# Attention lanes in fewer steps, another order of column groups, and VectorE's chunks of w_ada moved towards w_o

## The chip, the cores and the metric

The kernel runs on 1 core of one Trainium2 chip. The metric is the device time of one execution in microseconds (us); lower is better. The five engines of the core are TensorE (PE; its weight loads are listed apart as PEld), VectorE (DVE), ScalarE (ACT), GpSimd (POOL) and SyncE (SP, which only issues the DMA transfers here).

## The reference

Two transformer blocks run one after the other on x of 256 tokens by 2048 features, all in float32. The change lies in the first block alone:

```
mod = silu(c) @ w_ada + b_ada            # w_ada 2048 x 12288, six chunks of 2048: shift, scale, gate (twice)
h = rms_norm(x) * (1 + scale_a) + shift_a
proj = h @ w_in                          # 2048 x 5456: d_q, d_k, d_v, s_q, s_k, s_v, i_q, i_k, i_w
q, k, i_q, i_k = partial_rope(...)       # rotates the first quarter of each head
diff_out = rms_norm((softmax(q1 k1') - lam * softmax(q2 k2')) v)      # 8 heads, causal
dsa_out  = softmax over the top 64 keys of each query, by the indexer's scores   # 8 heads
x = x + gate_a * rms_norm([diff_out, dsa_out] @ w_o)
x = x + gate_f * rms_norm((silu(h w_gate) * (h w_up)) w_down)
```

The second block (w_in_2, MLA attention, a gated convolution, w_o_mla_2, w_o_conv_2, w_out_2) is not touched.

## The kernel before

**Chunks.** Every weight matrix is streamed from HBM in chunks of 512 rows by 512 columns (1 MB, four row blocks of 128). `chunk_plan` (from L52) writes the order of all chunks by hand. SP loads chunk c into slot c mod 5 of `raw` as soon as the slot's last chunk has been consumed (L2460 and what stands around it). A chunk of kind "lin" is used in two units (halves). For each unit ACT writes `whi`, the weights rounded to fp32r (L1039), DVE writes `wlo`, the remainder (L1648), and PE makes 12 matmuls from the pair (L566, L567, L568: hi by hi, lo by hi, hi by lo). ACT and DVE work two units ahead of PE (`AHEAD`), and there are three buffers for the pair (`NHL`), so that whi of unit i waits until PE has done unit i-3.

**w_ada.** The product with `silu(c)` is a vector times a matrix. The chunks of the column groups in `ADA_ON_PE` are multiplied on PE. Those of groups 8 to 19 ("ada" chunks here), four for each group, are multiplied and added up by DVE in `ada_step`: four instructions of 128x512 for each chunk (L1628, L1631) and one sum for each group (L1640). They are laid between the lin chunks: `BETWEEN` and `BETWEEN_LAST` say how many follow each of the first column groups of w_in, and `more` in `chunk_plan` spreads the others by `W_IN_SHARE` (over the 24 chunks of `W_IN_ORDER`) and `W_O_SHARE` (over w_o). When a group has been summed, `take` hands it to PE (L501, L502 or L506) and DVE (`mod`: L1610, L1612).

**First block.** w_in's column groups 10, 8, 9, 0, 2 are run first, a quarter of the rows at a time (`WIN_ITEMS`; DVE adds each quarter up in L1786). Then follow six column groups with all rows (`W_IN_ORDER`), then w_o. What follows the projection is done in lanes, generators that each engine's program advances by one step after each unit (`Walk.tick`). Lane 0 holds the indexer and the sparse attention of head pairs (0, 1), then (2, 3), lane 1 the differential attention of heads 0 to 3, then 4 to 7. `lane_jobs` says which column groups each needs before it is started. All engines walk through the same steps, each with its own work in them. The steps for one item of `attention` are: scores (PE L650, L653), maxima and exponentials (DVE L1874, L1876; ACT L1168), combine (DVE L2042 to L2048) with the turn of the next item, the transposes of the exponentials (PE L663 to L665, copied by ACT L1061 and DVE L1918), weigh (PE L673 to L676). Then comes finish (DVE L2057 copies a differential head out of PSUM to P1, after which ACT squares it in L1263; DVE L2021 for a sparse pair). Ahead of an attention stand the rotations (`rope`, DVE L1862 to L1865), two multiplications by the cosines and two by the sines, a difference and a sum, done for each token half (tb) by itself, a step for each.

w_o needs the lanes' results. Where they are not there, `Walk.until` runs steps with no unit beside them ("empty steps" here). The code of it in the tensor program:

```
need.wait_ge(m.s_dnorm, k.until(("d", 0)))
mix_operand(0, k.spare())
...
linear("w_o", 512, 512, ..., ks=(0,), s=sets[1], end=False)
linear("w_o", 0, 512, ..., ks=(8,), s=sets[0], begin=False, end=False)
need.wait_ge(m.s_dnorm, k.until(("d", 4)))
linear("w_o", 512, 512, ..., ks=(8,), s=sets[1], begin=False, end=False)
```

`mix_operand` turns a quarter of the attention's result (PE L582) and splits it (ACT L1084/L1086, DVE L1684/L1686). After each group of w_o's columns `post_group` squares it (ACT L1300) and multiplies it by the gate (DVE L2095).

## Time and profile before

| | |
|---|---|
| median of 3 runs | 2469.38 us (2468.66 to 2470.6) |
| the profiled execution, its time | 2470.69 us |
| its span | 2469.3 us |
| granted TensorE clock, mean | 0.969 |
| PE busy | 2314.2 us (94%) |
| DVE busy | 1408.0 us (57%) |
| ACT busy | 1059.2 us (43%) |
| DMA | 505.68 MB, mean 205 GB/s |

"Span" is the time from the first to the last instruction. "Busy" is the time in which an engine executes. The profile's waits name the instruction that waited, the one that released it, and the sum, count and longest of the waits. The clock of a stretch is the share of 2.4 GHz that was granted: 1.00 is 2.4 GHz throughout, 0.50 is 1.2 GHz, what lies between is a mixture of the two.

### The profile page before, as it was taken

The page shows a single profiled execution, that of the slowest core. Times are in us where ns is not written, and L with a number is a line of the kernel's source. Part 1 is how long each engine was busy: PE and PEld are TensorE (multiplying, and loading weights), DVE is VectorE, ACT ScalarE, POOL GpSimd, SP SyncE. Part 2 cuts the span into 40 slices and gives each one's busy share as a digit, 9 for nine tenths or more (in the row PEclk, how much of TensorE's full clock was granted, in tenths as well). Part 3 has the DMA queues.
Part 4 walks back from the last instruction along what each step waited for, and adds up shares of the span by engine and source line. Part 5 has one row for each costly group of instructions (what it writes and reads, how often), then busy time and mean ns, then how long its engine had stood idle before and what let it go on. Part 6 is the DMA issues. An engine that isn't in the chain of part 4 may idle for free.

```text
span 2469.3 us, 26356 instructions
## 1 busy us (share of the span) xinstructions
PE 2314.2 (94%) x10768; PEld 1875.1 (76%) x10768; DVE 1408.0 (57%) x1963; ACT 1059.2 (43%) x1461; POOL 0.7 (0%) x5
## 2 busy tenths in 40 slices
PE   5888968888999999999999899999999999999998
PEld 2665657666878888888888787888888888888886
DVE  1459888666667455455445554545554554554554
ACT  2422434434443444443444555555434444444443
POOL 0000000000000000000000000000000000000000
PEclk8998989888999999999999999999999999999999
DMA  8888757645577566555555464544565556556553
GB/s 300 336 318 301 247 197 265 219 156 185 184 275 264 198 233 213 187 193 195 188 188 191 142 195 145 162 145 154 174 200 189 188 183 197 187 187 200 188 187 138
DMA packets 255454, 505.68 MB, mean 205 GB/s; under 512 B 9077, under 2 KB 19662, under 8 KB 254182
## 3 DMA queue, kind: packets, MB, share of 16 engines
q1 hardware_dynamic: 255334, 504.00, 60.8%
q8 instruction: 85, 1.39, 0.2%
q14 instruction: 35, 0.29, 0.0%
HBM read 499.77 MB, written 4.19 MB: 204 GB/s over the span
## 4 chain that ended last, share of the span: by engine, by line
PE 82%; DVE 10%; ACT 3%; DMA 3%; issue 2%; SPq 0%; DVEq 0%; ACTq 0%
PE bank L566 25%; PE bank L568 25%; PE bank L567 25%; DVE wlo L1648 3%; DVE acc L1631 3%; PE bank L582 2%; PE bank L650 1%; DMA raw<-in_w_in_dram 1%; DMA raw<-in_w_ada_dram 1%; ACT whi L1039 1%; PE bank L520 1%; PE bank L590 1%; DVE x L1700 0%; DVE isc L1970 0%; ACT Ex_b L1168 0%
## 5 line engine op out<-in xcount | busy, mean ns | idle before, releaser
L1648 DVE TENSOR_TENSOR wlo<-raw,whi 128x1024 fp32r<-128x1024 f32 (+2 forms) x760 | 911.7, 1205 | 906.0 <-ACT whi L1039 905.4
L1039 ACT ACTIVATE whi<-raw 128x1024 fp32r<-128x1024 f32 (+2 forms) x760 | 790.2, 1044 | 1055.8 <-PE bank L568 954.0
L566 PE MATMUL bank<-whi,Ahi 128*128 128x512 f32 (+2 forms) x2304 | 916.0, 398 | 37.0 <-DVE wlo L1648 21.5
L567 PE MATMUL bank<-wlo,Ahi 128*128 128x512 f32 (+2 forms) x2304 | 900.8, 391 | 0.0
L568 PE MATMUL bank<-whi,Alo 128*128 128x512 f32 (+2 forms) x2304 | 900.2, 391 | 0.0
L566 PEld LDWEIGHTS bank<-whi,Ahi 128*128 128x128 f32 x2304 | 440.5, 191 | 142.1 <-DVE wlo L1648 30.4
L568 PEld LDWEIGHTS bank<-whi,Alo 128*128 128x128 f32 x2304 | 439.6, 191 | 91.1
L567 PEld LDWEIGHTS bank<-wlo,Ahi 128*128 128x128 f32 x2304 | 440.9, 191 | 84.5
L1631 DVE SCALAR_TENSOR_TENSOR acc<-raw,cs,acc 128x512 f32<-128x512 f32 x224 | 153.1, 746 | 0.0
L566 PE MATMUL bank<-whi,Fhi 128*128 128x512 f32 x352 | 137.7, 391 | 0.0
L568 PE MATMUL bank<-whi,Flo 128*128 128x512 f32 x352 | 137.0, 389 | 0.0
L567 PE MATMUL bank<-wlo,Fhi 128*128 128x512 f32 x352 | 137.0, 389 | 0.0
L566 PE MATMUL bank<-whi,Bhi 128*128 128x512 f32 x256 | 101.1, 395 | 0.0
L568 PE MATMUL bank<-whi,Blo 128*128 128x512 f32 x256 | 99.8, 390 | 0.0
L567 PE MATMUL bank<-wlo,Bhi 128*128 128x512 f32 x256 | 99.7, 390 | 0.0
L566 PEld LDWEIGHTS bank<-whi,Fhi 128*128 128x128 f32 x352 | 66.1, 188 | 14.1 <-issue 0.8
L568 PEld LDWEIGHTS bank<-whi,Flo 128*128 128x128 f32 x352 | 66.1, 188 | 14.0
L567 PEld LDWEIGHTS bank<-wlo,Fhi 128*128 128x128 f32 x352 | 66.1, 188 | 13.6
L568 PEld LDWEIGHTS bank<-whi,Blo 128*128 128x128 f32 x256 | 48.1, 188 | 10.3
L520 PE MATMUL bank<-raw,cs 128*32 128x512 f32 x256 | 37.6, 707 | 19.4 <-DMA raw<-in_w_ada_dram 19.4
L566 PEld LDWEIGHTS bank<-whi,Bhi 128*128 128x128 f32 x256 | 48.1, 188 | 10.0 <-issue 0.3
L567 PEld LDWEIGHTS bank<-wlo,Bhi 128*128 128x128 f32 x256 | 48.1, 188 | 9.6
(291 smaller groups left out, 1372.8 us busy)
## 6 DMA issues: line engine op xcount, KB each, us to landing
raw<-in_w_in_dram SPq DMA_DIRECT2D x156, 1024.0 KB, 5.0
raw<-in_w_ada_dram SPq DMA_DIRECT2D x96, 1024.0 KB, 5.1
raw<-in_w_gate_dram SPq DMA_DIRECT2D x44, 1024.0 KB, 5.1
raw<-in_w_up_dram SPq DMA_DIRECT2D x44, 1024.0 KB, 5.1
raw<-in_w_down_dram SPq DMA_DIRECT2D x44, 1024.0 KB, 5.0
raw<-in_w_o_dram SPq DMA_DIRECT2D x16, 1024.0 KB, 5.4
raw<-in_w_o_mla_dram SPq DMA_DIRECT2D x16, 1024.0 KB, 4.9
raw<-in_w_o_conv_dram SPq DMA_DIRECT2D x16, 1024.0 KB, 4.9
```

Source lines behind the costliest of these rows:

```text
L520: ins = pe.matmul(m.bank[b][32 * jj:32 * jj + 32, :], m.cs32[:, 4 * j + jj, :], m.raw[:, c % NRAW, jj, :], start=(j == 0), stop=(j == 3))
L566: pe.matmul(o, a_hi, w_hi, start=beg, stop=False)
L567: pe.matmul(o, a_hi, w_lo, start=False, stop=False)
L568: ins = pe.matmul(o, a_lo, w_hi, start=False, stop=fin)
L582: ins = pe.matmul(o, i, m.diag[:, tb, :], start=True, stop=True) if scaled else pe.transpose(o, i, m.ident)
L590: ins = pe.transpose(m.bank[b][:, tb * P:tb * P + P], src(tb), m.ident)
L650: pe.matmul(m.bank[ln.bank[mm]][:, PART[tb]], l, r, start=(i == 0), stop=False, skip_group_check=True)
L1039: act.activation(m.whi[:, i % NHL, :, 0:n], m.raw[:, c % NRAW, 2 * h:2 * h + 2, 0:n], ACT.Copy).then_inc(m.s_hi, 1)
L1631: ins = dve.scalar_tensor_tensor(out=o, in0=w, scalar=col, in1=o, op0=ALU.mult, op1=ALU.add)
L1648: dve.tensor_tensor(m.wlo[:, i % NHL, :, 0:n], m.raw[:, c % NRAW, 2 * h:2 * h + 2, 0:n], m.whi[:, i % NHL, :, 0:n].bitcast(F32), ALU.subtr ...
```

## The change

1. `rope` rotates both token halves in one instruction instead of one each; it takes one step where there were two, and the scratch tile `rt` grows from 256 to 272 columns for it. The two small copies of the indexer (w32, ik2) are merged in the same way.
2. The lanes have fewer steps ahead of the attention: the indexer 2 instead of 5, sparse 1 instead of 3, differential 2 instead of 5.
3. A differential head is copied out of PSUM by ACT (in `finish`, ahead of its squares) and no longer by DVE.
4. `W_IN_ORDER` becomes 4, 6, 1, 3, 5, 7.
5. `BETWEEN_LAST` goes from (2, 2, 2, 2, 2) to (1, 1, 1, 1, 2), `W_IN_SHARE` from 28 to 26, `W_O_SHARE` from 10 to 15. Of the 48 ada chunks of groups 8 to 19, 10 were in the last quarter of the first column groups, 28 in `W_IN_ORDER` and 10 in w_o. Now it is 6, 26 and 16.
6. `post_group` waits for the gate columns of its own group alone.

The diff, with what the steps above name:

```
@@ -35,11 +35,11 @@
 ROW = 2048
 
 W_IN_FIRST = (10, 8, 9, 0, 2)
-W_IN_ORDER = (4, 1, 6, 3, 5, 7)
-
-BETWEEN, BETWEEN_LAST = (3, 3, 2, 0, 0), (2, 2, 2, 2, 2)
-W_IN_SHARE = 28
-W_O_SHARE = 10
+W_IN_ORDER = (4, 6, 1, 3, 5, 7)
+
+BETWEEN, BETWEEN_LAST = (3, 3, 2, 0, 0), (1, 1, 1, 1, 2)
+W_IN_SHARE = 26
+W_O_SHARE = 15
 THIRDS = ((0, 4), (4, 8), (8, 11))
 
 
@@ -415,7 +415,7 @@
         self.skT = sb("skT", [P, S])
         self.rl = sb("rl", [P, 768])
         self.sqj = sb("sqj", [P, P])
-        rt = sb("rt", [P, 4, 256])
+        rt = sb("rt", [P, 4, 272])
         self.lane = [Lane(sb, "a", rt, (4, 5), sem), Lane(sb, "b", rt, (6, 7), sem)]
         self.ik2 = self.isc[:, 0, :].rearrange("p (t a d) -> p t a d", t=2, a=2)
         self.iwk = self.rl[:, 0:S]
@@ -711,11 +711,8 @@
         b0, b1 = ln.bank
         yield
         yield
-        yield
-        yield
-        yield
-        need.wait_ge(ln.s_rope, 4)
-        for _ in range(4):
+        need.wait_ge(ln.s_rope, 2)
+        for _ in range(2):
             k.up(ln.s_rope)
         turn_pair(b0, lambda tb: m.P1[:, tb, C_SK:C_SK + 128])
         need.wait_ge(m.s_ik, 1)
@@ -749,9 +746,7 @@
 
     def sparse(i, pairs):
         ln = m.lane[i]
-        for _ in range(2):
-            rope = k.up(ln.s_rope)
-            yield
+        rope = k.up(ln.s_rope)
         yield
         while "bias" not in k.mixed:
             yield
@@ -774,10 +769,9 @@
     def differential(i, heads):
         ln = m.lane[i]
         lo = heads[0]
-        for _ in range(4):
+        for _ in range(2):
             rope = k.up(ln.s_rope)
             yield
-        yield
 
         def turn(h):
             need.wait_ge(ln.s_rope, rope)
@@ -1216,7 +1210,7 @@
     def indexer(i):
         ln = m.lane[i]
         b0, b1 = ln.bank
-        for _ in range(5):
+        for _ in range(2):
             yield
         sk, ik = k.use(b0), k.use(b1)
         yield
@@ -1240,11 +1234,10 @@
         k.mixed["bias"] = True
 
     def sparse(i, pairs):
+        yield
+        while "bias" not in k.mixed:
+            yield
         ln = m.lane[i]
-        for _ in range(3):
-            yield
-        while "bias" not in k.mixed:
-            yield
         yield from attention(ln, pairs, 128 ** -0.5, 2, lambda hp: 8, lambda hp, pv: None)
         for hp in pairs:
             k.mixed["s", hp] = ln.bank[1], k.uses[ln.bank[1]]
@@ -1252,12 +1245,14 @@
     def differential(i, heads):
         ln = m.lane[i]
         lo, hi = heads[0], heads[-1] + 1
-        for _ in range(5):
+        for _ in range(2):
             yield
 
         def finish(h, pv):
-            need.wait_ge(m.freed[ln.bank[1]], pv)
+            b = ln.bank[1]
             c0 = C_DQ + 128 * h
+            copy_out(m.P1[:, :, c0:c0 + 128], b, pv, m.bank[b][:, 0:256].rearrange("p (t d) -> p t d", t=2))
+            need.wait_ge(m.freed[b], pv)
             for tb in range(2):
                 need.wait_ge(m.s_a, a.n)
                 a.up(act.activation(m.sqj[:, :], m.P1[:, tb, c0:c0 + 128], ACT.Square, accum_out=m.ss16[:, tb, h, 0:1]))
@@ -1848,15 +1843,14 @@
     need.wait_ge(m.s_shlo, 8)
     rt_at = [(m.s_lam, 1)]
 
-    def rope(tb, c0, h, d, half_d, tcol, ln, *cgs):
+    def rope(c0, h, d, half_d, tcol, ln, *cgs):
 
         for cg in cgs:
             released(*k.P_at[cg])
-        x = m.P1[:, tb, c0:c0 + h * d].rearrange("p (h d) -> p h d", d=d)
-        x1, x2 = x[:, :, 0:half_d], x[:, :, half_d:2 * half_d]
-        c = m.cos[:, tb, tcol:tcol + half_d].unsqueeze(1).broadcast_to([P, h, half_d])
-        sn = m.sin[:, tb, tcol:tcol + half_d].unsqueeze(1).broadcast_to([P, h, half_d])
-        r = [ln.rt[:, i, 0:h * half_d].rearrange("p (h d) -> p h d", d=half_d) for i in range(4)]
+        x = m.P1[:, :, c0:c0 + h * d].rearrange("p t (h d) -> p t h d", d=d)
+        x1, x2 = x[:, :, :, 0:half_d], x[:, :, :, half_d:2 * half_d]
+        c, sn = (t[:, :, tcol:tcol + half_d].unsqueeze(2).broadcast_to([P, 2, h, half_d]) for t in (m.cos, m.sin))
+        r = [ln.rt[:, i, 0:2 * h * half_d].rearrange("p (t h d) -> p t h d", t=2, d=half_d) for i in range(4)]
         need.wait_ge(*rt_at[0])
         for o, p1, p2 in ((r[0], x1, c), (r[1], x2, sn), (r[2], x2, c), (r[3], x1, sn)):
             v.up(dve.tensor_tensor(o, p1, p2, ALU.mult))
@@ -1900,7 +1894,7 @@
         for n, h in enumerate(items):
             if taken:
                 mod(*taken)
-            if n:
+            if n and finish:
                 finish(items[n - 1], (n - 1) % 2, sc, pv)
             sc = k.use(b0), k.use(b1)
             yield
@@ -1925,28 +1919,20 @@
             yield
         if taken:
             mod(*taken)
-        finish(items[-1], (len(items) - 1) % 2, sc, pv)
+        if finish:
+            finish(items[-1], (len(items) - 1) % 2, sc, pv)
 
     def indexer(i):
         ln = m.lane[i]
         b0, b1 = ln.bank
-        for tb in range(2):
-            rope(tb, C_IQ, 17, 64, 8, 0, ln, 8, 9, 10)
-            yield
-        for tb in range(2):
-            rope(tb, C_SK, 1, 128, 16, 8, ln, 8)
-        yield
-        for tb in range(2):
-            v.up(dve.tensor_scalar(m.w32[:, tb, :], m.P1[:, tb, C_IW:C_IW + 16], 1.0 / 32.0, None, ALU.mult))
-        need.wait_ge(ln.s_rope, 4)
-        for tb in range(2):
-            for j in range(2):
-                ins = dve.tensor_copy(m.ik2[:, tb, j, :], m.P1[:, tb, C_IK:C_IK + 64])
-                if tb + j < 2:
-                    v.up(ins)
-        ins.then_inc(m.s_ik, 1)
+        rope(C_IQ, 17, 64, 8, 0, ln, 8, 9, 10)
+        yield
+        rope(C_SK, 1, 128, 16, 8, ln, 8)
+        v.up(dve.tensor_scalar(m.w32[:, :, :], m.P1[:, :, C_IW:C_IW + 16], 1.0 / 32.0, None, ALU.mult))
+        need.wait_ge(ln.s_rope, 2)
+        dve.tensor_copy(m.ik2[:, :, :, :], m.P1[:, :, C_IK:C_IK + 64].unsqueeze(2).broadcast_to([P, 2, 2, 64])).then_inc(
+            m.s_ik, 1)
         settle()
-        yield
         yield
         k.use(b0), k.use(b1)
         yield
@@ -2005,9 +1991,7 @@
 
     def sparse(i, pairs):
         ln = m.lane[i]
-        for tb in range(2):
-            rope(tb, C_SQ + 256 * pairs[0], 2 * len(pairs), 128, 16, 8, ln, 6 + pairs[0] // 2)
-            yield
+        rope(C_SQ + 256 * pairs[0], 2 * len(pairs), 128, 16, 8, ln, 6 + pairs[0] // 2)
         yield
         while "bias" not in k.mixed:
             yield
@@ -2029,11 +2013,9 @@
         ln = m.lane[i]
         lo, hi = heads[0], heads[-1] + 1
         cg = lo // 4
-        for tb in range(2):
-            for c0 in (C_DQ, C_DK):
-                rope(tb, c0 + 128 * lo, 2 * len(heads), 64, 8, 0, ln, cg, 2 + cg)
-                yield
-        yield
+        for c0 in (C_DQ, C_DK):
+            rope(c0 + 128 * lo, 2 * len(heads), 64, 8, 0, ln, cg, 2 + cg)
+            yield
 
         def combine(slot, sc):
 
@@ -2051,15 +2033,11 @@
                     v.up(ins)
             ins.then_inc(ln.s_cb, 1)
 
-        def finish(h, slot, sc, pv):
-            b = ln.bank[1]
-            need.wait_ge(m.filled[b], pv)
-            dve.tensor_copy(m.P1[:, :, C_DQ + 128 * h:C_DQ + 128 * h + 128],
-                            m.bank[b][:, 0:256].rearrange("p (t d) -> p t d", t=2)).then_inc(m.freed[b], 1)
-
-        yield from attention(ln, heads, 0.125, 1, lambda h: 4 + cg, combine, finish)
+        yield from attention(ln, heads, 0.125, 1, lambda h: 4 + cg, combine, None)
+        at = ln.bank[1], k.uses[ln.bank[1]]
         yield
         need.wait_ge(m.s_ssq, k.up(m.s_ssq))
+        released(at)
         v.up(dve.reciprocal(m.ss16[:, :, lo:hi, 0], m.ss16[:, :, lo:hi, 1]))
         settle()
         for tb in range(2):
@@ -2116,10 +2094,12 @@
     y_at = []
     for g in (0, 1):
         s = linear("w_o", 512 * g, 512, ks=(12,), s=sets[g])
-        released(*(mod_at[j] for j in range(8, 12)))
+        released(mod_at[8 + g])
         y_at += post_group(m.y1, g, s)
     for g in (2, 3):
-        y_at += post_group(m.y1, g, linear("w_o", 512 * g, 512))
+        s = linear("w_o", 512 * g, 512)
+        released(mod_at[8 + g])
+        y_at += post_group(m.y1, g, s)
     k.take_rest()
     rms_both()
     released(*y_at)
```

## Rows read from the trace of the kernel before

**Rows 1.** Stretches: start:end, length, busy PE/PEld/DVE/ACT/POOL, clock, DMA share, GB/s.

```profile
179.00:230.00 51.00, 40.08 (x139) 27.61 (x138) 49.08 (x95) 11.66 (x11) 0.00 (x0) 0.87 0.89 310
230.00:448.00 218.00, 185.01 (x893) 143.82 (x891) 189.78 (x405) 86.71 (x186) 0.00 (x0) 0.91 0.72 247
448.00:484.40 36.40, 27.80 (x131) 22.07 (x131) 25.86 (x55) 16.06 (x40) 0.00 (x0) 0.86 0.58 194
484.40:515.60 31.20, 18.40 (x91) 14.38 (x89) 9.43 (x31) 11.37 (x41) 0.00 (x0) 0.65 0.10 34
515.60:597.00 81.40, 79.36 (x356) 65.14 (x356) 57.93 (x71) 32.21 (x42) 0.00 (x0) 0.97 0.71 246
```

**Rows 2.** Waits from 179 to 448: waiting line, its releaser, sum, times, longest.

```profile
DVE wlo L1648 <- ACT whi L1039: 21.6, 13, 2.7
...
ACT sqj L1263 <- DVE P L2057: 26.3, 5, 14.3
...
PE bank L650 <- DVE P L2057: 15.0, 2, 11.3
```

**Rows 3.** Timeline of DVE: start, duration, line and tiles, count [idle before it].

```profile
214.15 0.29 DVE L1862 TENSOR_TENSOR rt<-P,cos 128x136 f32<-128x136 f32 x1
214.36 0.29 DVE L1862 TENSOR_TENSOR rt<-P,sin 128x136 f32<-128x136 f32 x1
...
236.88 2.73 DVE L1631 SCALAR_TENSOR_TENSOR acc<-raw,cs,acc 128x512 f32<-128x512 f32 x4
239.71 0.69 DVE L1640 TENSOR_TENSOR acc<-acc 128x512 f32<-128x512 f32 x1
240.32 1.22 DVE L1648 TENSOR_TENSOR wlo<-raw,whi 128x1024 fp32r<-128x1024 f32 x1
241.46 0.22 DVE L1862 TENSOR_TENSOR rt<-P,cos 128x64 f32<-128x64 f32 x1
241.59 0.22 DVE L1862 TENSOR_TENSOR rt<-P,sin 128x64 f32<-128x64 f32 x1
...
242.40 1.22 DVE L1648 TENSOR_TENSOR wlo<-raw,whi 128x1024 fp32r<-128x1024 f32 x1
...
307.15 0.41 DVE L2057 COPY P<-bank 128x256 f32<-128x256 f32 x1
```

**Rows 4.** Timeline of PE inside the empty steps.

```profile
499.52 0.49 PE L673 MATMUL bank<-P,ET_a 128*128 128x128 f32 x2 [2.37 <-ACT ET_a L1061]
...
502.20 2.07 PE L650 MATMUL bank<-skT,qT_a 128*128 128x256 f32 x4 [0.85 <-DVE P L2021]
```

**Rows 5.** Timeline of DVE and ACT in the last of the empty steps.

```profile
505.88 1.15 DVE L1874 TENSOR_REDUCE sm_a<-bank 128x1 f32<-128x128 f32 x4 [3.73 <-PE bank L653]
...
507.27 0.47 ACT L1168 ACTIVATE Ex_a<-bank,sm_a 128x256 f32<-128x256 f32 x1 [7.80 <-DVE sm_a L1876]
...
508.87 0.50 ACT L1061 ACTIVATE ET_b<-bank 128x384 f32<-128x384 f32 x1
...
512.42 1.28 ACT L1268 ACT_TABLE_LOAD   x1
...
514.05 0.20 DVE L2063 RECIPROCAL ss<-ss 128x8 f32<-128x8 f32 x1 [2.52 <-ACT ss L1268]
```

**Rows 6.** Timeline of DVE in w_o, with ada chunks, and later without.

```profile
552.83 1.28 DVE L2095 TENSOR_TENSOR P<-bank,G 128x512 f32<-128x512 f32 x2
554.03 2.73 DVE L1631 SCALAR_TENSOR_TENSOR acc<-raw,cs,acc 128x512 f32<-128x512 f32 x4
...
558.95 2.73 DVE L1631 SCALAR_TENSOR_TENSOR acc<-raw,cs,acc 128x512 f32<-128x512 f32 x4
...
568.52 1.23 DVE L1648 TENSOR_TENSOR wlo<-raw,whi 128x1024 fp32r<-128x1024 f32 x1 [2.37 <-ACT whi L1039]
...
573.96 1.23 DVE L1648 TENSOR_TENSOR wlo<-raw,whi 128x1024 fp32r<-128x1024 f32 x1 [1.44 <-ACT whi L1039]
```

**Rows 7.** Busy time by stretch, inside w_o, columns as in the first group.

```profile
540.00:560.00 20.00, 19.21 (x84) 15.25 (x84) 19.05 (x27) 9.46 (x16) 0.00 (x0) 1.00 0.94 340
```

More of the change, by code:

```diff
@@ L37 @@
 W_IN_FIRST = (10, 8, 9, 0, 2)
-W_IN_ORDER = (4, 1, 6, 3, 5, 7)
-BETWEEN, BETWEEN_LAST = (3, 3, 2, 0, 0), (2, 2, 2, 2, 2)
-W_IN_SHARE = 28
-W_O_SHARE = 10
+W_IN_ORDER = (4, 6, 1, 3, 5, 7)
+BETWEEN, BETWEEN_LAST = (3, 3, 2, 0, 0), (1, 1, 1, 1, 2)
+W_IN_SHARE = 26
+W_O_SHARE = 15
 THIRDS = ((0, 4), (4, 8), (8, 11))
@@ L713, in indexer @@
         yield
-        yield
-        yield
-        yield
-        need.wait_ge(ln.s_rope, 4)
-        for _ in range(4):
+        need.wait_ge(ln.s_rope, 2)
+        for _ in range(2):
             k.up(ln.s_rope)
@@ L751, in sparse @@
         ln = m.lane[i]
-        for _ in range(2):
-            rope = k.up(ln.s_rope)
-            yield
+        rope = k.up(ln.s_rope)
         yield
@@ L776, in differential @@
         lo = heads[0]
-        for _ in range(4):
+        for _ in range(2):
             rope = k.up(ln.s_rope)
             yield
-        yield
         def turn(h):
@@ L1218, in indexer @@
         b0, b1 = ln.bank
-        for _ in range(5):
+        for _ in range(2):
             yield
@@ L1242, in sparse @@
     def sparse(i, pairs):
-        ln = m.lane[i]
-        for _ in range(3):
-            yield
+        yield
         while "bias" not in k.mixed:
             yield
+        ln = m.lane[i]
         yield from attention(ln, pairs, 128 ** -0.5, 2, lambda hp: 8, lambda hp, pv: None)
@@ L1254, in differential @@
         lo, hi = heads[0], heads[-1] + 1
-        for _ in range(5):
+        for _ in range(2):
             yield
         def finish(h, pv):
-            need.wait_ge(m.freed[ln.bank[1]], pv)
+            b = ln.bank[1]
             c0 = C_DQ + 128 * h
+            copy_out(m.P1[:, :, c0:c0 + 128], b, pv, m.bank[b][:, 0:256].rearrange("p (t d) -> p t d", t=2))
+            need.wait_ge(m.freed[b], pv)
             for tb in range(2):
@@ L1902, in attention @@
                 mod(*taken)
-            if n:
+            if n and finish:
                 finish(items[n - 1], (n - 1) % 2, sc, pv)
@@ L1927, in attention @@
             mod(*taken)
-        finish(items[-1], (len(items) - 1) % 2, sc, pv)
+        if finish:
+            finish(items[-1], (len(items) - 1) % 2, sc, pv)
     def indexer(i):
@@ L1932, in indexer @@
         b0, b1 = ln.bank
[L1933 to L1947 removed]
+        rope(C_IQ, 17, 64, 8, 0, ln, 8, 9, 10)
+        yield
+        rope(C_SK, 1, 128, 16, 8, ln, 8)
+        v.up(dve.tensor_scalar(m.w32[:, :, :], m.P1[:, :, C_IW:C_IW + 16], 1.0 / 32.0, None, ALU.mult))
+        need.wait_ge(ln.s_rope, 2)
+        dve.tensor_copy(m.ik2[:, :, :, :], m.P1[:, :, C_IK:C_IK + 64].unsqueeze(2).broadcast_to([P, 2, 2, 64])).then_inc(
+            m.s_ik, 1)
         settle()
[L1949 removed]
         yield
@@ L2007, in sparse @@
         ln = m.lane[i]
-        for tb in range(2):
-            rope(tb, C_SQ + 256 * pairs[0], 2 * len(pairs), 128, 16, 8, ln, 6 + pairs[0] // 2)
-            yield
+        rope(C_SQ + 256 * pairs[0], 2 * len(pairs), 128, 16, 8, ln, 6 + pairs[0] // 2)
         yield
@@ L2031, in differential @@
         cg = lo // 4
-        for tb in range(2):
-            for c0 in (C_DQ, C_DK):
-                rope(tb, c0 + 128 * lo, 2 * len(heads), 64, 8, 0, ln, cg, 2 + cg)
-                yield
-        yield
+        for c0 in (C_DQ, C_DK):
+            rope(c0 + 128 * lo, 2 * len(heads), 64, 8, 0, ln, cg, 2 + cg)
+            yield
         def combine(slot, sc):
@@ L2052, in combine @@
             ins.then_inc(ln.s_cb, 1)
-        def finish(h, slot, sc, pv):
-            b = ln.bank[1]
-            need.wait_ge(m.filled[b], pv)
-            dve.tensor_copy(m.P1[:, :, C_DQ + 128 * h:C_DQ + 128 * h + 128],
-                            m.bank[b][:, 0:256].rearrange("p (t d) -> p t d", t=2)).then_inc(m.freed[b], 1)
-        yield from attention(ln, heads, 0.125, 1, lambda h: 4 + cg, combine, finish)
+        yield from attention(ln, heads, 0.125, 1, lambda h: 4 + cg, combine, None)
+        at = ln.bank[1], k.uses[ln.bank[1]]
         yield
         need.wait_ge(m.s_ssq, k.up(m.s_ssq))
+        released(at)
         v.up(dve.reciprocal(m.ss16[:, :, lo:hi, 0], m.ss16[:, :, lo:hi, 1]))
@@ L2118, in vector_program @@
         s = linear("w_o", 512 * g, 512, ks=(12,), s=sets[g])
-        released(*(mod_at[j] for j in range(8, 12)))
+        released(mod_at[8 + g])
         y_at += post_group(m.y1, g, s)
     for g in (2, 3):
-        y_at += post_group(m.y1, g, linear("w_o", 512 * g, 512))
+        s = linear("w_o", 512 * g, 512)
+        released(mod_at[8 + g])
+        y_at += post_group(m.y1, g, s)
     k.take_rest()
```

28 lines of the change are left out of this document (6 added, 22 removed).

## The prediction

> **What bounds the kernel now.** I read the busy time by stretch first. The stretches that the change touches lie between 179 and 597 us [rows 1]; what stands before and behind them is left as it is. From 179 to 230 (the last quarter of the first column groups, 10 ada chunks) DVE is busy for 49.1 of 51 us, and PE runs at a mean clock of 0.87. From 230 to 448 (the 24 chunks of `W_IN_ORDER`, 28 ada chunks) DVE is busy for 189.8 of 218 us. What PE has to do there for w_in is 48 units at 2.72 us, 131 us (two units without ada chunks beside them take 573.96-568.52 = 5.44 [rows 6]); the rest of the stretch is lane work and waiting. DVE waits for almost one thing only, ACT's whi, 21.6 us [rows 2]. So the first 269 us go at the pace of DVE, whatever it does is on the path, and other engines' waits there are its queue seen from outside: PE waits 15.0 us and ACT 26.3 us for the copy of a head that stands in DVE's queue behind other work [rows 2].
>
> From 448 to 515.6 w_o's first six units are run, and then, from 484.4, nothing but lane steps: 31.2 us with DVE busy for 9.4 and DMA at a share of 0.10 [rows 1]. There the chain of one lane step after another is the bound. From 515.6 PE is (79.4 of 81.4 us), with DVE at 57.9 [rows 1].
>
> **Counting the steps.** I counted the lane steps from the code, one step for each unit. Before, the differential lane of heads 4 to 7 still lacks 8 steps when `until(("d", 4))` is reached, which makes 8 empty steps, 31.2/8 = 3.9 us each [rows 1]. With either order this lane can start once column groups 1 and 3 are there, 16 units before w_in's end, so its 3 steps fewer count in full. One more goes because before, the lane is held up for a step by the hand-over of a summed group, and after it isn't. That leaves 4 empty steps. The sparse lane of pairs (2, 3) starts at w_in's end in both and has 2 steps fewer. The order 4, 6, 1 only keeps the first sparse lane from waiting behind the shorter indexer for group 6 (with 1 before 6 it would start one step later); I give it 0.
>
> **Part A, 179 to 230: -11.5 us.** Four ada chunks go. One is 4 instructions in 2.7 us, less their overlap with the next, 2.65, and a quarter of the group's sum, 0.61/4 = 0.15 us [rows 3], so 2.8 us; 4 x 2.8 = 11.2. The indexer's rotations are merged: see below, 0.5. What is left is 39 us of DVE. PE needs 10 units, 27 us. DMA moved 15.8 MB (310 GB/s in 51 us) and needs 4 MB less, 11.6 MB, which in 39 us is 298 GB/s, less than the 310 that it gave. DVE remains the bound, and the gain is whole. Bounds: -4 us, if the transfers went at the 247 GB/s of the next stretch (11.6 MB in 47 us), and -13 us, if DVE's last idle 2 us went too.
>
> **Part B, 230 to 448: -9 us.** Two ada chunks, 5.6 us. Five pairs of rotations of 64 columns: one takes 242.40-241.46 = 0.94 us, its instructions start 0.13 us apart; at 136 columns they start 0.21 us apart [rows 3]. So a column costs 0.08/72 = 1.1 ns and an instruction 0.06 to 0.07 us by itself. A merged rotation of 128 columns is then 6 x 0.20 + 0.2 (its two waits for itself) = 1.4 us instead of 1.88, and the five pairs give 2.5 us. Five heads' copies leave DVE, 0.35 us each (0.41, a little of it beside the next instruction [rows 3]), 1.7 us. ACT takes them over, and is busy for 86.7 of 218 us, ahead of squares for which it now waits for DVE: its copy hides there; if it didn't, 8 x 0.4 = 3 us. Against it stand one more maxima (1.4 us) because the lane of heads 4 to 7 is further on when w_in ends, and one gate multiplication that comes from part A (0.6 us, as the sum of the same size [rows 3]). Sum: 5.6 + 2.5 + 1.7 - 2.0 = 7.8 us. PE's wait of 11.3 us for a copy goes as well [rows 2], but PE isn't the bound, and DVE was busy in the meantime; only of DVE's own 21.6 us can it give something back. I take 1 of them. Bounds: -4 us (the ada chunks alone, with a part of them turned into waits for whi) and -20 (half of the 21.6 us on top).
>
> The Trainium skill (VectorE: DVE Perf Modes, The TRN2 errata) has a fixed cost of 151 cycles, 157 ns, for each fp32 tensor_tensor, paid between instructions, by which the 48 instructions that merging removes would be 7.5 us over the kernel. The durations agree (0.22 and 0.29 us), but the starts lie closer than the durations [rows 3], so the rows leave some 3.3 us of it; the sum goes by the starts.
>
> **Part C, 448 to 515.6: -9 us.** The four empty steps that are left hold, in order: the wait for combine of head 7, for which I estimate 4 us (behind the scores DVE has an ada chunk, two wlo, maxima for two lanes and combine to do, 2.7 + 2.3 + 2.6 + 1.9 = 9.5 us and some waiting for ACT, against PE's two units and a turn, 6.5 us); the transposes and their copies, 1.2; weigh and the pair's finish, 502.20-499.52 = 2.7 [rows 4], and 0.9 for the second lane; scores of pair 3, 3.7 (502.20 to 505.88); maxima 1.4, exponentials 1.6, table load and root 1.6, reciprocal and product 1.6 [rows 5]. The sum is 18.7 us against 31.2, -12.5. The removed steps' work isn't gone. The scores of pair 2, 3.7 us of PE, now stand between w_o's first units, and the chunk plan puts two ada chunks ahead of unit 88's wlo, behind which combine of head 6 is queued on DVE; for that PE's transposes wait, which I put at 2 us of the 2.8 that the second chunk takes. Of the 5.7 some 2 fall into idle time of PE (36.4 - 27.8 = 8.6 us in the stretch to 484.4 [rows 1]). +3.5, so -9. Bounds: -3 and -15.6 (four steps at 3.9 us and nothing in return).
>
> **Part D, w_o, 515.6 to 597: +3 us.** Behind the empty steps come 13 lin chunks, with 7 ada chunks among them before and 12 after. DVE makes a lin and an ada chunk in 558.95-554.03 = 4.92 us, a group's post_group takes 554.03-552.83 = 1.2 [rows 6]; over four chunks that is 4 x 4.92 + 0.6 + 1.2 + 0.2 = 21.7 us against PE's 21.8. It just fits, and each unevenness shows. The queue that is moved past is SP's too: 2.1 MB in 5.44 us are 385 GB/s, and where that pattern stands now, DMA is at 340 GB/s with a share of 0.94, PE busy for 19.2 of 20 us [rows 7]. 340/0.94 = 362 GB/s, so a pair could take 5.8 us, 12 x 0.36 = 4 us, less what the five slots hold at the start. I take +3; bounds 0 and +14 (five more chunks of 2.8 us wholly exposed). The mix_operand of the last quarter loses its slack of two units behind the sparse lane's finish: below 1 us, in the 3. The last group's sum is taken one chunk before w_o's end, so the normalization behind w_o meets nothing new. The narrower wait of post_group was met before and gives 0.
>
> The Trainium skill (Perfetto Trace Analysis, Engine Utilization) gives 358 GB/s as the peak for a core; by that rule a pair takes 5.86 us and part D costs 12 x 0.42 = 5 us rather than 3. The row above, 340 at 0.94, doesn't speak against it.
>
> **Sum.** -11.5 - 9 - 9 + 3 = -26.5 us. The profiled execution took 2470.69 us (span 2469.3), the median of the runs is 2469.38, 1.3 lower. 2470.7 - 26.5 = 2444.2, and as a median 2443 us.
>
> **The rivals.**
> 1. Loops shorten too. With DVE's queue shorter and the copies on ACT, the waits for each other shrink as well: of the 21.6 us half goes, and part C comes near its bound, -11 - 4. Time 2428. For it: DVE waits for ACT, and ACT and PE wait for DVE [rows 2], so a shorter queue shortens all three. Against it: most of the 13 waits for whi are those of an exponential ahead of whi on ACT (longest 2.7), and these steps stay. Chance 0.13.
> 2. w_o takes it back. DVE or the transfers are late in w_o, and part D costs its bound of 14 instead of 3, part B gives 5. Time 2443 + 11 + 4 = 2458. For it: 21.7 against 21.8 and 385 against 362 GB/s. Chance 0.16.
> 3. The saved DVE time turns into waits for whi: the three buffers tie DVE to PE, PE to the lanes' steps, and the steps' chain has its own pace; A gives 6, B 0, C 3, D costs 7. Time about 2467. DVE's 96% in A speaks against it. Chance 0.04.
> 4. Slower: a lin and an ada chunk have a pace of their own, through slots and transfers. In `W_IN_ORDER` a chunk with its ada chunk takes 218/24 = 9.1 us. If that is the pair's pace and not the lane work's, each pair more in w_o costs 9.1 - 5.44 = 3.7 us, 6 x 3.7 = 22; A then gives its bound of 4 and B nothing, and C nothing either, since each of its four steps that stand beside units meets a slower pair (4 x 3.7 = 15 us against 12.5). The time is 2469 - 4 + 22 = 2487. It decides from a pair time of 7.9 us in w_o, where 12 pairs x 2.46 us eat the 29.5 us of A, B and C. DVE's pair of 4.92 us speaks against it [rows 6], and so does PE's 96% beside such pairs [rows 7]. Chance 0.03.
>
> The forecast itself has 0.64: its own range is 2432 to 2454. A measurement of this kernel can tell some 0.2% (5 us) from no change, so below 2464.4 is faster: 0.64 + 0.13 + 0.16 = 0.93. Within 0.2%: 0.04; slower: 0.03. The range of 8 in 10 reaches a little into the second rival and into the first: 2428 to 2458.
>
> **What would show it.** Right: no idle of PE at L650 behind a head's copy; the stretch of empty steps is 17 to 21 us long; DVE still over 90% busy in the last quarter of the first groups, which takes 38 to 41 us; w_in's end some 20 us earlier than 448; w_o's last 26 units in 82 to 86 us with DVE near 90%. Wrong: DVE's waits for whi before w_in's end grow by more than 8 us; PE waits for wlo in w_o by more than 5 us in sum; ACT becomes the releaser of PE's longest waits.

## The result, and the profile after

The changed kernel takes 2428.15 us (median, 2425.32 to 2429.59) against 2469.02 us (2467.12 to 2470.6) in the same comparison: ratio 0.9833, 95% interval 0.9816 to 0.985. The forecast was 2443; the result is 15 us below it, at the edge of the range, where the first rival had put its time. The profiled execution took 2428.22 us, its span is 2426.9 against 2469.3.

To compare the two, I cut both traces where DVE starts the same `wlo`, since these mark the same units of work in both. The stretches are: A (the last quarter of the first column groups), B (`W_IN_ORDER`), C1 (w_o's first chunks up to the empty steps), C2 (the empty steps, with one unit), D (the rest of w_o). The kernel before on this cut, columns as in [rows 1]:

```profile
175.90:224.60 48.70, 39.07 (x137) 26.98 (x135) 46.62 (x77) 11.53 (x12) 0.00 (x0) 0.86 0.83 286
224.60:445.20 220.60, 186.32 (x897) 145.12 (x898) 192.73 (x422) 88.17 (x185) 0.00 (x0) 0.91 0.73 248
445.20:482.40 37.20, 28.60 (x135) 22.57 (x134) 27.03 (x61) 15.75 (x38) 0.00 (x0) 0.86 0.63 213
482.40:518.20 35.80, 22.97 (x106) 18.09 (x105) 13.21 (x37) 12.07 (x44) 0.00 (x0) 0.66 0.11 36
518.20:593.10 74.90, 72.89 (x334) 59.90 (x334) 52.92 (x67) 31.15 (x41) 0.00 (x0) 0.98 0.74 254
```

And the changed kernel, the same five stretches:

```profile
177.80:213.90 36.10, 31.60 (x138) 23.77 (x137) 35.67 (x61) 13.07 (x15) 0.00 (x0) 1.00 0.80 271
213.90:417.00 203.10, 180.43 (x900) 140.35 (x900) 184.67 (x371) 92.80 (x203) 0.00 (x0) 0.96 0.76 260
417.00:459.70 42.70, 34.60 (x159) 27.21 (x160) 28.68 (x58) 17.01 (x46) 0.00 (x0) 0.81 0.61 208
459.70:476.70 17.00, 9.37 (x60) 7.74 (x59) 9.21 (x24) 7.14 (x21) 0.00 (x0) 0.83 0.19 63
476.70:553.90 77.20, 73.15 (x345) 60.03 (x344) 65.75 (x88) 31.55 (x42) 0.00 (x0) 0.99 0.85 302
```

| stretch | before | after | difference | forecast |
|---|---|---|---|---|
| up to A (not touched) | 175.9 | 177.8 | +1.9 | 0 |
| A | 48.7 | 36.1 | -12.6 | -11.5 |
| B | 220.6 | 203.1 | -17.5 | -9 |
| C1 and C2 | 73.0 | 59.7 | -13.3 | -9 |
| D | 74.9 | 77.2 | +2.3 | +3 |
| behind D (not touched) | 1876.2 | 1873.0 | -3.2 | 0 |

The sum is -42.4, as the spans have it. The miss is in B (8.5 us) and C (4.3 us). In B, DVE's busy time fell by 192.73 - 184.67 = 8.1 us, which is the work that the forecast had counted (7.8). But its idle time fell too, from 27.9 to 18.4 us, and that is 9.4 us where the forecast had 1. Behind D, which the change doesn't touch, the profiled executions of all kernels took between 1872.4 and 1877.1 us, so the 3.2 us there are no effect of the change that these runs could show. The waits of the changed kernel from 177.8 to 417 (columns as in [rows 2]):

```profile
DVE wlo L1643 <- ACT whi L1033: 14.7, 9, 2.7
...
PE bank L663 <- DVE Ex_b L2030: 12.9, 2, 8.8
```

DVE's wait for whi went from 21.6 us in 13 waits to 14.7 in 9. Another wait of B went altogether; this is the kernel before, from 224.6 to 445.1, DVE waiting to take over a group of `modT` that PE sums:

```profile
DVE modT L1612 <- PE bank L506: 2.5, 1, 2.5
```

PE's wait at L650 behind a head's copy (15.0 us before) is gone from B. Its longest is now for combine's `Ex_b`, 8.8 us: DVE's queue seen from outside again, in another place.

The empty steps, seen on PE in the changed kernel (start, duration, line; idle before it in brackets):

```profile
460.27 0.60 PE L590 MATMUL bank<-const,P 128*128 128x128 f32 x4
...
462.90 0.33 PE L663 MATMUL bank<-const,Ex_b 128*128 128x128 f32 x1 [0.91 <-DVE Ex_b L2030]
...
463.46 0.46 PE L673 MATMUL bank<-P,ET_a 128*128 128x128 f32 x2
...
466.36 1.11 PE L650 MATMUL bank<-skT,qT_a 128*128 128x256 f32 x4
...
474.70 0.79 PE L566 MATMUL bank<-whi,Ahi 128*128 128x512 f32 x1 [6.45 <-DVE P L2045]
```

and their end on DVE:

```profile
468.35 1.15 DVE L1868 TENSOR_REDUCE sm_a<-bank 128x1 f32<-128x128 f32 x4 [1.66 <-PE bank L653]
...
473.11 0.20 DVE L2041 RECIPROCAL ss<-ss 128x8 f32<-128x8 f32 x1 [3.40 <-ACT ss L1263]
```

From 460.3 to 474.7 there are 14.4 us, against 31.2 before [rows 1] and 18.7 in the forecast.

w_o behind them runs as the forecast had it. In this stretch of the changed kernel PE is never idle, and the transfers reach 377 GB/s, close to the 385 that a pair in 5.44 us asks for:

```profile
520.00:540.00 20.00, 20.00 (x94) 16.68 (x93) 17.94 (x25) 8.59 (x11) 0.00 (x0) 1.00 1.02 377
```

### The profile page after: what moved, and what is told of

Read it like the earlier page. It is cut to its first block, busy times and chain, and to the rows that moved or that the text cites. A ratio compares the mean times of both kernels' runs of the same rounds, so it can differ in the third digit from the quotient of the medians.

```text
span 2426.9 us, 26309 instructions
## 1 busy us (share of the span) xinstructions
PE 2291.2 (94%) x10768; PEld 1861.1 (77%) x10768; DVE 1399.5 (58%) x1903; ACT 1062.3 (44%) x1469; POOL 0.7 (0%) x5
## 4 chain that ended last, share of the span: by engine, by line
PE 82%; DVE 10%; ACT 3%; DMA 3%; issue 2%; SPq 0%; DVEq 0%; ACTq 0%
PE bank L566 26%; PE bank L568 25%; PE bank L567 25%; DVE wlo L1643 3%; DVE acc L1626 2%; PE bank L582 2%; DMA raw<-in_w_in_dram 2%; ACT whi L1033 1%; PE bank L650 1%; DMA raw<-in_w_ada_dram 1%; PE bank L520 1%; PE bank L590 1%; DVE x L1695 0%; ACT Ex_b L1162 0%; PE bank L673 0%
## 5 line engine op out<-in xcount | busy, mean ns | idle before, releaser
L567 PEld LDWEIGHTS bank<-wlo,Fhi 128*128 128x128 f32 x352 | 66.1, 188 | 13.4
L520 PE MATMUL bank<-raw,cs 128*32 128x512 f32 x256 | 35.9, 681 | 21.3 <-DMA raw<-in_w_ada_dram 21.3
```

The costliest lines, as they stand in the source:

```text
L520: ins = pe.matmul(m.bank[b][32 * jj:32 * jj + 32, :], m.cs32[:, 4 * j + jj, :], m.raw[:, c % NRAW, jj, :], start=(j == 0), stop=(j == 3))
L567: pe.matmul(o, a_hi, w_lo, start=False, stop=False)
```

## The experiments

All ratios are to the kernel before. The whole change has 0.9833, and once more 0.9829 (0.9816 to 0.9843) in a second comparison. "The rest" below means the merged rotations with the fewer steps, the new order and the narrower wait of `post_group`. B, its DVE idle time (the length of B less DVE's busy time in it) and C2, in us, are cut as above, each from the one profiled execution of that kernel.

| kernel | ratio | B | DVE idle in B | C2 |
|---|---|---|---|---|
| before | 1 | 220.5 | 27.9 | 35.8 |
| copy alone | 0.9972 | 218.0 | 27.1 | 36.5 |
| rest alone | 0.9924 | 218.3 | 27.6 | 20.9 |
| shares alone | 0.9875 | 215.5 | 26.1 | 25.3 |
| shares and copy | 0.9866 | 210.7 | 22.9 | 28.7 |
| copy and rest | 0.9909 | 211.1 | 22.2 | 21.3 |
| shares and rest | 0.9857 | 208.9 | 22.4 | 16.9 |
| all (after) | 0.9833 | 203.1 | 18.4 | 16.9 |

**The copy taken back** (shares and rest):

```
-            copy_out(m.P1[:, :, c0:c0 + 128], b, pv, ...)     # in finish of ACT
+            dve.tensor_copy(m.P1[:, :, ...], m.bank[b][:, 0:256] ...)   # in finish of DVE
```

> The changed kernel, but DVE copies a differential head out of PSUM again, as before. Theory 1 (the waits between the engines went because the copy left DVE's queue, where PE's scores stood behind it): up to the end of w_in DVE's waits for whi come back by some 7 us and its work by 2, PE waits at L650 for the copy again; 9 us slower than the changed kernel, 0.987 to 0.988 of before. Theory 2 (the waits went because DVE had fewer chunks in its queue, whatever stood there): only the copy's own 2 to 3 us come back, 0.984 to 0.9845 of before.

Measured 0.9857 (0.9842 to 0.9872), 6 to 7 us slower than the change, between the two theories. DVE is busier by 1.9 us in B (186.54 against 184.67), its five copies, and idle for 3.9 us more. So in B the copy is worth three times its own time here, 5.8 us. The sum had only the copy's own time. PE does wait at L650 for the copy again (6.9 us), but DVE's waits for whi came back by 2.1 us only, not by the 7 of theory 1.

**The copy alone**, on the kernel before:

> The kernel before, with the copy of a differential head moved from DVE to ACT and nothing else. Theory 1: PE's 15 us of waits at L650 go, DVE's waits with them, -8 to -12 us, 0.995 to 0.997. Theory 2: 8 copies of 0.35 us leave DVE, -2 to -3 us, 0.999.

Measured 0.9972 (0.9963 to 0.9982), again between the two theories. PE's longest wait in B of this kernel:

```profile
PE bank L650 <- DVE modT L1614: 10.9, 1, 10.9
```

With one for `G` (L1612, 3.3 us) PE waits 14.2 us at L650. This is the wait that stood behind the copy before (15.0 us, longest 11.3 [rows 2]), nearly as long as ever and under another name. The kernel before shows why. There the hand-over of `modT` stands directly in front of the copy in DVE's queue:

```profile
342.36 0.16 DVE L1612 TENSOR_TENSOR modT<-bank,bT 128x4 f32<-128x4 f32 x1
342.44 0.41 DVE L2057 COPY P<-bank 128x256 f32<-128x256 f32 x1
```

The scores (their weight loads had waited 11.7 us for `modT`) began at 343.0 there and at 342.5 in the copy alone. The copy was only the last of what was late. DVE's idle time fell by 0.8 us.

**The shares alone**:

```
-BETWEEN, BETWEEN_LAST = (3, 3, 2, 0, 0), (2, 2, 2, 2, 2)
-W_IN_SHARE = 28
-W_O_SHARE = 10
+BETWEEN, BETWEEN_LAST = (3, 3, 2, 0, 0), (1, 1, 1, 1, 2)
+W_IN_SHARE = 26
+W_O_SHARE = 15
```

> The kernel before, with the new BETWEEN_LAST, W_IN_SHARE and W_O_SHARE alone. Sum of the prediction for the chunks: -11.2 in the last quarter of the first groups, -5.6 in W_IN_ORDER, +3 to +4 in w_o, -13 us, 0.9945. Theory 2 adds 7 us of waits: -20 us, 0.992. If w_o took back more than was measured in the changed kernel (+3.7), the difference shows at w_o's end.

Measured 0.9875 (0.986 to 0.9889), -31 us where 13 were expected, or 20 by theory 2; both lie outside the interval. A gave 13.1, B 5.0 (its two chunks are 5.6), D took 0.7. The surprise is C2, 35.8 to 25.3 us, although by my count only one lane step went (the hand-over of group 14 no longer holds the lane up).

**The shares taken back** (copy and rest):

> The changed kernel with the old BETWEEN_LAST, W_IN_SHARE and W_O_SHARE. Theory 1: what is left are lanes and copy, -27 us against before, 0.989. Theory 2: -20 us, 0.992.

Measured 0.9909 (0.9893 to 0.9926), -22.5 us, against -31 for the shares alone: together 53.5, while the whole change gives 41. The two overlap in C2 (-14.5 and -10.5 alone, -18.9 together) and help each other in B (-9.4 and -5.0 alone, -17.4 together). The profiled execution of this kernel took 2437.58 us, the three others 2445.91 to 2450.39, so the stretches read from it are less certain than those of the other kernels.

**The order taken back**, `W_IN_ORDER = (4, 1, 6, 3, 5, 7)`, all else as changed:

> The changed kernel with the old W_IN_ORDER (4, 1, 6, 3, 5, 7). By the count of steps the first sparse lane starts one step later and nothing else moves: within 2 us of the changed kernel, 0.983 to 0.984 of before. The rival, that the alignment of the sparse lane's steps with the differential lane's sets the loops' waits: 5 us or more either way.

Measured 0.985 (0.9826 to 0.9874); B 205.7, DVE idle 21.1. So the order, which I gave 0, is worth some 2.6 us in B. The time alone can't be told from the change's.

**The steps taken back**: rotations merged, with empty `yield`s where the halves had theirs, on all engines:

```
         rope = k.up(ln.s_rope)
+        yield
+        yield
         yield
         while "bias" not in k.mixed:
```

> The changed kernel with as many lane steps as before (indexer 5, sparse 3, differential 5), the rotations still merged, the copy still on ACT, the chunk plan new. 7 empty steps instead of 4. The step theory (each lane step that is removed is worth its 3.5 us at the end, and nothing before w_in's end): +10 us over the changed kernel, 0.987. The rival (the end costs what the two lanes' alignment makes it, as the plan-only kernel showed with 21 us for 7 steps): +6 to +8, 0.9857 to 0.9865.

Measured 0.9841 (0.9827 to 0.9856), below both expectations (the rival's 0.9857 lies just outside the interval): with 7 empty steps instead of 4, only some 2 us are lost. C2 is 28.5 instead of 16.9 us, but C1 is 35.6 instead of 42.8. The steps that the change moves out of the empty stretch are paid for between w_o's first units, at 7.2 of 11.6 us. I had 3.5 of 12.5.

**The rotations split in token halves again**, within the new steps:

> The changed kernel with each rotation done for the two token halves one after the other again, in the same step (48 DVE instructions more). By the starts of the instructions in the trace of before, 0.5 us for each of 8 pairs, 7 of them where DVE is the bound: +3.5 to 4 us, 0.985. By the Trainium skill's fixed cost of 157 ns for each instruction: +7.5 us, 0.9865. If merging is worth nothing: 0.9833.

Measured 0.9851 (0.9837 to 0.9866), some 5 us slower. DVE is busier by 1.3 us in A, 2.9 in B and 0.5 in C1, 4.7 in all, 98 ns for each of the 48 instructions. The sum by the distance of the starts had 0.5 in A and 2.5 in B; in A it left out the indexer's second, smaller pair of rotations. The merged form itself is as forecast, 0.20 us from start to start (331.12, 331.32 in the changed kernel).

By the fixed cost of the Trainium skill (VectorE: DVE Perf Modes, The TRN2 errata), 151 cycles or 157 ns, the 48 instructions are an estimated 7.5 us. This run shows 4.7 us of DVE's time for them, so neither that estimate nor my 3.3 us was right.

**PE's wait for the differential lane put behind the next chunk's matmuls**, on PE alone, so that the steps stay as they are:

```
-    need.wait_ge(m.s_dnorm, k.until(("d", 4)))
+    d4 = k.until(("d", 4))
     linear("w_o", 512, 512, m.A_op, mixed, ks=(8,), s=sets[1], begin=False, end=False)
+    need.wait_ge(m.s_dnorm, d4)
```

> The changed kernel, with PE's wait for the normalized heads 4 to 7 moved behind the chunk of w_o that does not need them (rows 8 to 11 of w_o, second column group), in front of the turn that does. In the trace of the changed kernel PE stood 6.5 us at that wait with two units' weights ready; they would cover some 5 of it. -4 to -6 us, 0.981. If the chain of DVE and ACT simply ends later because of it: 0.983.

Measured 0.9824 (0.9809 to 0.9839). The time can't be told from the change itself (0.9829 and 0.9833), nor from the 0.981 of the expectation. The stretches of the profiled execution do tell them apart. C2 and D:

```profile
456.70:473.60 16.90, 14.55 (x92) 12.01 (x90) 9.19 (x24) 9.34 (x24) 0.00 (x0) 1.00 0.19 63
473.60:546.10 72.50, 68.10 (x311) 55.75 (x312) 65.68 (x89) 29.15 (x39) 0.00 (x0) 0.98 0.90 321
```

C2 is as long as in the changed kernel, with 5.2 us more of PE's work in it, and D is 4.7 us shorter than the 77.2 of the changed kernel. That is the gain that was expected; 2.8 us of it are taken back behind D, where executions differ by as much. So in this execution PE's wait at the end of the empty steps was covered for the most part, which the change leaves undone.

**The wait moved a whole chunk later, on all engines** (`until(("d", 4))` behind the chunk in PE's, ACT's and DVE's program), beside **the changed kernel once more**:

> The changed kernel once more, as the measure for the others of this group. 0.9833 was measured; anything from 0.982 to 0.985 agrees with it. Its stages in the first profile: B (unit 40 to 88) 203.1 us, empty steps 16.9 us, DVE idle in B 18.4 us. If the idle of DVE in B were chance of one execution, it would differ by several us here; if it belongs to the program, it stays within 2 us.

> The changed kernel with the wait for the differential lane moved behind the next w_o chunk (rows 8 to 11, group 1) in all programs: two of the four empty steps become steps beside two units. By my count of PE's work the two units, 5.4 us, leave PE's stretch behind and fill a stretch in which PE idles for most of its time. Theory (the chain of the lanes' steps has room beside it): -4 us against the changed kernel, 0.9817. Rival (the lane's steps on DVE stand behind wlo of these units and the chain is longer by what it saves behind): 0.983 to 0.984, no gain. It could also be slower by a few us if the head's exponentials wait behind whi of both units.

Measured 0.9837 (0.9823 to 0.985) against 0.9829. C2 shrinks to 5.1 us, and D grows from 77.2 to 88.1. C1 to D are 136.2 us in this kernel and 136.5 in the repeated change. PE's wait for DVE's product (L2045), 6.5 us in the changed kernel, has moved with it to L582 and takes 6.4 us.

Putting a whole chunk beside the lane's last steps on all engines gains nothing: the lane ends later by as much. On PE alone, in the run before this one, it took 4.7 us off D. That the chunk's work on ACT and DVE is what holds the lane up fits both runs but was not read from either. The repeated run answers the other question. B is 203.1 us again, DVE's idle time 18.5, C2 16.9, D 77.2; B is also 203.4 us in the kernel with PE's late wait and 203.0 in the one above, whose edits both lie behind B. What happens in these stretches belongs to the program, not to one execution.

**One ada chunk moved**, in the kernel before, everything else as it was:

```
-BETWEEN, BETWEEN_LAST = (3, 3, 2, 0, 0), (2, 2, 2, 2, 2)
+BETWEEN, BETWEEN_LAST = (3, 3, 2, 0, 0), (2, 2, 2, 2, 1)
-W_O_SHARE = 10
+W_O_SHARE = 11
```

> The kernel before with one ada chunk moved: the last column group of the last quarter has 1 instead of 2, and w_o spreads its 11 over 11 chunks instead of 10 over 10. By the count of lane steps the hand-over of group 14 then falls elsewhere, and 7 empty steps remain instead of 8. Alignment theory (one step less brings the scores of head 7 out of step with combine of the sparse lane, and the stretch falls from 35.7 to 25 to 28 us, as it did with the whole plan): -2.8 for the chunk and -8 to -10 for the stretch, ratio 0.995 to 0.9957. Plain count (a step is 3.9 us wherever it stands, as my prediction had it): -2.8 - 3.9, ratio 0.9973. Rival (the stretch fell with the plan because of the work that is no longer beside it, not because of the step): -2.8 alone, 0.9989, and the stretch stays at 35 us.

Measured 0.9939 (0.9926 to 0.9953): one chunk of 2.8 us gives 15 us. These are B and C2 of this kernel, to be read against the 220.60 us, 186.32 (x897) and the 35.80 us, 22.97 (x106) above:

```profile
220.00:443.70 223.70, 188.01 (x912) 147.13 (x913) 193.64 (x427) 90.80 (x196) 0.00 (x0) 0.92 0.71 242
...
480.10:505.90 25.80, 14.49 (x80) 11.88 (x79) 12.40 (x37) 10.59 (x39) 0.00 (x0) 0.70 0.22 79
```

26 of PE's 106 matmuls have left C2, and PE is busy for 8.5 us less, of the 10.0 by which it is shorter. PE's idle time there hardly changed (12.8 and 11.3 us). So a step removed is not worth the mean of 3.9 us. It is worth what the two lanes together then no longer have to do there. That work is not gone: the 26 matmuls turn up in B (15 more), C1 (4) and D (7), and B is 3.1 us longer, with DVE idle for 30.1 us and its waits for whi at 26.5 us. The gain of A is 4.2 us, DVE's 2.7 of work and 1.5 of its idle time. The plain count (0.9973) and the rival (0.9989) both lie outside the interval; of the alignment theory's 0.995 to 0.9957 the lower end lies inside. The shares alone show the same stretch (25.3 us, x80).

**Shares and copy**:

> The kernel before with the new shares and with the head's copy on ScalarE; rotations, steps and order as before. The shares alone made B 215.5 us, the copy alone took 2.5 from B. Pair theory (shares and copy together are what removes DVE's idle time in B; it fell from 27 to 18 us in the changed kernel and in no version with one of the two alone): B about 207, DVE idle 20, ratio 0.985. Additive: B 213, ratio 0.9865. Crowd theory (any third part does it as well as the copy): between them.

Measured 0.9866 (0.9852 to 0.9879), the additive theory's ratio. But B is 210.7 and DVE's idle time 22.9, between the two theories' numbers (207 and 213 for B), and C2 takes some of it back, with 28.7 us against the 25.3 of the shares alone. **The rest alone** completes the eight combinations:

> The changed kernel with the shares of before and the head's copy back on VectorE: only the merged rotations, the fewer steps and the new order are left. The other seven combinations are measured. DVE's idle time in B: 27.9 before, 26.1 with the shares alone, 27.1 with the copy alone, 22.4 with shares and rest, 22.2 with copy and rest, 22.9 with shares and copy, 18.4 with all. Additive theory (each part takes its own wait away; the rest's own is 4 to 5): idle 23.5, B 214 us, total like the kernel with shares of before (0.9909) plus 1.9 us of copies and 2 of waits, 0.9925. Together theory (a part alone gives 1 to 2): idle 26 to 27, B 217, 0.994.

Measured 0.9924 (0.9909 to 0.9939): idle 27.6 and B 218.3, as the "together" theory had them. The total met the additive one's number, but for another reason, C2 (20.9 us with 5 empty steps). The table then reads plainly. Any one part alone takes 0.3 to 1.8 us off DVE's idle time. Any two take 5.0 to 5.7. All three take 9.4. B itself, with the work that goes from it, falls in the same way: by 2.2 to 5.0 us for one part, 9.4 to 11.6 for two, 17.4 for three. The parts in "the rest" were not taken apart in this table; the order's own share is the 2.6 us of the run above.

**Two chunks taken back, and one more moved**, both from the changed kernel:

```
BETWEEN_LAST (1, 1, 1, 2, 2), W_IN_SHARE 27, W_O_SHARE 13
BETWEEN_LAST (1, 1, 1, 1, 1), W_IN_SHARE 26, W_O_SHARE 16
```

> The changed kernel with two ada chunks taken back from w_o, one for the last quarter of the first column groups and one for W_IN_ORDER. By the count 5 empty steps instead of 4. Plain count: +2.8 in A, +2.8 in B, +3.9 for the step, -1 in w_o: +8.5, ratio 0.9867. Alignment theory (the price of a step depends on what stands beside it, so anything between 0 and 10 us): the empty stretch is not 16.9 + 3.9 but lies anywhere from 17 to 27 us, and B moves by other than 2.8.

Measured 0.9901 (0.9884 to 0.9917), 17 us slower than the change for two chunks of 2.8. The plain count (0.9867) lies outside the interval. A is 2.6 us longer and C2 23.8 us, within what the alignment theory left open; most of the loss is in B. B of this kernel, with one chunk more than after:

```profile
214.80:430.30 215.50, 191.96 (x910) 149.13 (x911) 187.04 (x375) 92.51 (x201) 0.00 (x0) 0.91 0.72 248
```

DVE is busy for 2.4 us more and idle for 28.5 us instead of 18.4. Of these 10.1 us 9.5 are in three waits: for whi 17.6 us instead of 14.7, 1.9 us at L2005 for PE's weighed values, which the changed kernel doesn't have in B, and this one, which it doesn't have either:

```profile
DVE modT L1607 <- PE bank L506: 4.7, 1, 4.7
```

> The changed kernel with one more ada chunk moved from the last quarter to w_o (16 instead of 15 chunks share them). Empty steps by the count: 4 as in the changed kernel. Theory (A goes at DVE's pace): A -2.8, w_o has one more pair, +0.5 to +2.8, so -1 +- 1.5: 0.9825. Rival (A is no longer DVE's: DVE is busy for 35.7 of 36.1 us there, PE for 31.6, so 4 us of room remain; against it DMA at 272 GB/s): the same. If hand-over places matter here too, the total moves by more than 3 us one way or the other though the number of steps is the same.

Measured 0.9834 (0.982 to 0.9849), the same as the change. A gave 2.6 us (33.5), as DVE's pace there would have it. B took 1.9 back with the same 26 chunks in it, C1 and C2 2.6. So the gain of A was lost behind it with the same number of empty steps. That the places of the hand-overs did it isn't shown: the total moved by less than the 3 us that the expectation had named as the sign of it.

## Why the prediction missed

**The bound, and part A, hold.** A took 36.1 us (forecast 37.2 on this cut), with DVE busy for 35.67. In the kernel with one more chunk moved, A fell by another 2.6, as did DVE's busy time there. DVE's pace sets A, and a chunk is worth what it takes. The 12.6 us are 11 of DVE's work and 1.7 of its idle time (2.1 before, 0.4 after), which the forecast had as a bound. The 2.65 us for a chunk is not what its rows show: its first instruction and the one behind its fourth start 2.83 us apart [rows 3]. But a chunk moved out of A took 2.6 to 2.9 us of DVE's busy time in the runs, so the 2.8 in the sum was right.

**Part B: "I take 1 of them" is the step that failed.** The work was right (8.1 us of DVE's busy time against 7.8). What was wrong was to count the waits as fixed and each edit by itself: DVE's idle time fell by 9.4 us, not by 1. Each edit alone does behave so: 0.3 to 1.8 us of idle time. Any two take 5.0 to 5.7 and all three 9.4. The copy alone shows one such wait of PE: it went over to what stood directly in front of the copy in DVE's queue, at nearly the same length, so the sign "no idle of PE at L650 behind a head's copy" says nothing by itself. With shares and copy the longest wait at L650 is 7.7 us, and with all three there is none in B. That DVE's own waits shrink together for the same reason is argued from this; no run shows it for one of them. The 17.5 us of B lie within the bound of 20 that I had given.

The first rival had the mechanism (shorter queues shorten the waits on both sides) and nearly the size: it took half of 21.6 us; 9.4 us of idle time went, 6.9 of them in the waits for whi. I gave it 0.13, arguing that most waits for whi are those of an exponential ahead of whi on ACT, which stay. 9 waits did stay, where there had been 13; four and the one for `modT` went. That its time, 2428 us, was met exactly is partly luck. By the stretches, the result lies below the forecast by 8.5 us in B, where the rival had 11. In C it is 4.3 where the rival had 4, but for other causes (next paragraph), and the rest came from A (1.1), D (0.7) and the stretches that the change doesn't touch (1.3).

**Part C: two terms.** The step count can't be read off a trace, but the pieces can. The empty stretch held, in the forecast's order and in us: combine 4 (measured 2.6), transposes 1.2 (0.6), weigh and finish 3.6 (2.9), scores 3.7 (2.0), maxima 1.4 (1.4), exponentials and root 3.2 (3.4), reciprocal and product 1.6 (1.6). The tail on ACT and DVE was right. The scores were too long because I took them from the end of the empty steps before. There, from 502.2 to 515.6, PE was busy for 7.1 of 13.4 us and the granted clock was 0.50, its level of 1.2 GHz; the four score matmuls took 2.07 us [rows 4], while the same four had taken 1.03 at 484.4, behind w_o's matmuls. After, they took 1.11, in a stretch (466.3 to 474.7) with a mean clock of 0.78. Most pairs of weigh's matmuls took 0.39 us both times; what went there is PE's wait for DVE's `P`, 0.85 us before [rows 4]. Another 2.0 us of C went in the part of C2 outside these steps (35.8 - 31.2 before, 17.0 - 14.4 after). On the other side the lane work between w_o's first units cost more than my 3.5 us: C1 grew by 5.5. One piece of that are the weight loads of PE's scores (L650), which wait for DVE's `modT` for 4.9 us in C1, 2.4 before. Together C gave 13.3 instead of 9.

The price of 3.9 us for a step, from which my outer bound of C came, was not a property of a step. One chunk moved took one step and 10 us of C2; three steps taken back changed C2 by 11.6 us and the time by 2.

**Part D holds.** +2.3 on 24 units, forecast +3. The second rival, w_o taking it back, didn't happen. PE waits for wlo in D by 0.9 us in sum, as before (0.8). The pair's own pace was no bound (fourth rival): 377 GB/s were moved with PE busy throughout. The third didn't happen either: DVE's waits for whi in B fell. The Trainium skill (Perfetto Trace Analysis, Engine Utilization) gives 358 GB/s as a core's peak, which my 5 us for D by that rule took as a ceiling. But the same section says that this is the share when both cores of a pair use the memory, and that one core alone can reach about 120% of it. The row from 520 to 540 agrees with that: 377 GB/s, 105%, on the one core that runs here.

**The signs that I had named.** No idle of PE at L650 behind a head's copy: right. Empty steps 17 to 21 us: 14.4. DVE over 90% busy in A, A 38 to 41 us: 99%, 36.1. w_in's end some 20 us earlier: 28 us, from 445.2 to 417.0 on this cut. w_o's last units at 82 to 86, DVE near 90%: 79.2 (474.7 to 553.9), DVE 85% in D. None of the wrong signs appeared.

**What stays open.** That the idle time of B depends on where the lane steps, the ada chunks and the hand-overs meet is shown by the eight combinations and by the two neighbours of the plan. Which meeting each microsecond comes from isn't settled. The waits for whi and for `modT` make up the difference between before and after (6.9 + 2.5 of 9.4 us), and those for whi, `modT` and PE's weighed values that between after and the kernel with two chunks back (2.9 + 4.7 + 1.9 of 10.1 us). But why the plan's neighbour has them and the plan has not was read from no experiment.

## What to carry to other kernels

Where two engines wait for each other in a loop, price an edit's work and its waits apart, and don't keep the waits constant when several edits shorten the same queue: alone each may give only its work, together they give the waits as well. The idle time in such a loop then belongs in the range as one term (here 28 us), not as 1 us. A mean price of a step (stretch by number of steps) is no price. List what each engine does in the stretch, at the clock that it will have there, and try the neighbours of a hand-written plan: one chunk moved was worth 15 us once, two moved back cost 17 us another time, and one moved gave nothing a third time.
